# A first phase that takes the scale first and adds the shift to six of eight token tiles afterwards

## The reference, cut to what matters

```python
mod = jax.nn.silu(c) @ w_ada[l] + b_ada[l]
sh1, sc1, g1, sh2, sc2, g2 = [m[:, None, :] for m in jnp.split(mod, N_MOD, axis=-1)]
h = _rmsnorm(x, norm_g[l, 0]) * (1.0 + sc1) + sh1
z = h @ w_in
```

## Time and profile before

| | |
|---|---|
| median of 3 runs | 1763.02 us |
| lowest, highest | 1757.39, 1763.32 us |
| the profiled execution | 1760.8 us |
| its span, first to last instruction | 1759.0 us |
| PE busy | 1672.6 us, 95% |
| DVE busy | 1044.9 us, 59% |
| POOL busy | 821.6 us, 47% |
| ACT busy | 595.5 us, 34% |

### The profile page before, as it was taken

One profiled execution on the slowest core, in us unless ns is written; L12 is line 12 of the kernel. 1 busy time (PEld: TensorE's weight loads), 2 busy tenths in 40 slices (PEclk: granted clock), 3 DMA queues, 4 the chain that ended last, 5 costly groups with the idle time before them and its releaser, 6 DMA issues.

```text
span 1759.0 us, 22694 instructions
## 1 busy us (share of the span) xinstructions
PE 1672.6 (95%) x8036; PEld 1394.4 (79%) x8036; DVE 1044.9 (59%) x1746; ACT 595.5 (34%) x1054; POOL 821.6 (47%) x537
## 2 busy tenths in 40 slices
PE   2899999999999999989999999999999999999996
PEld 2787878787888888879888788888888888888884
DVE  5714835656999999947577345743453354345438
ACT  1533336264222222246323354323223222322323
POOL 0621130102446565520388423766558556755664
PEclk9999999998999999999999999999999999999998
DMA  8222141010111111240674511121112011201213
GB/s 288 86 60 60 40 110 42 31 36 32 47 58 45 45 45 51 105 102 1 221 271 160 203 61 48 37 72 48 48 48 72 25 63 55 65 30 48 72 69 158
DMA packets 37166, 138.87 MB, mean 79 GB/s; under 512 B 4592, under 2 KB 4592, under 8 KB 37104
## 3 DMA queue, kind: packets, MB, share of 16 engines
q1 hardware_dynamic: 34864, 130.70, 21.7%
q0 software_dynamic: 2240, 7.34, 1.9%
HBM read 118.10 MB, written 13.63 MB: 75 GB/s over the span
## 4 chain that ended last, share of the span: by engine, by line
PE 80%; DVE 8%; DMA 4%; issue 3%; ACT 3%; POOL 2%; SPq 0%; DVEq 0%; POOLq 0%; ACTq 0%
PE ps L612 23%; PE ps L614 23%; PE ps L613 23%; PE ps L811 4%; PE ps L790 2%; DMA region_b<-in_w_ada 2%; DVE y_f L2179 1%; PE ps L716 1%; DVE y_f L2148 1%; PE ps L717 1%; DVE region_a L2133 1%; ACT y_t L1407 1%; PE ps L642 1%; DMA raw<-in_w_ffn 1%; DVE region_a L2206 1%
## 5 line engine op out<-in xcount | busy, mean ns | idle before, releaser
L612 PE MATMUL ps<-h_t,w_t 128*128 128x512 f32 x1112 | 437.4, 393 | 0.6 <-POOL w_t L1500 0.4
L614 PE MATMUL ps<-h_t,w_t 128*128 128x512 f32 x1112 | 433.6, 390 | 0.0
L613 PE MATMUL ps<-h_t,w_t 128*128 128x512 f32 x1112 | 433.5, 390 | 0.0
L612 PEld LDWEIGHTS ps<-h_t,w_t 128*128 128x128 f32 x1112 | 209.4, 188 | 45.2 <-issue 2.4
L614 PEld LDWEIGHTS ps<-h_t,w_t 128*128 128x128 f32 x1112 | 209.2, 188 | 44.1
L613 PEld LDWEIGHTS ps<-h_t,w_t 128*128 128x128 f32 x1112 | 209.4, 188 | 42.9 <-issue 0.7
L1500 POOL TENSOR_TENSOR w_t<-raw,w_t 128x1280 fp32r<-128x1280 f32 (+1 forms) x50 | 141.6, 2832 | 196.0 <-ACT w_t L1097 195.7
L2148 DVE TENSOR_TENSOR y_f<-ps,y_f 128x512 f32<-128x512 f32 x120 | 80.7, 686 | 217.5 <-PE ps L614 217.5
L1649 POOL TENSOR_TENSOR w_t<-raw,w_t 128x512 fp32r<-128x512 f32 x80 | 110.2, 1383 | 144.5 <-ACT w_t L1388 144.4
L1833 DVE MAX8 top<-region_b 128x8 f32<-128x384 f32 (+5 forms) x192 | 157.9, 881 | 17.3 <-issue 16.7
L1836 DVE MATCH_REPLACE8 region_b<-top,region_b 128x384 f32<-128x384 f32 (+5 forms) x192 | 166.1, 876 | 0.0
(11 more groups left out here) (266 smaller groups left out, 3264.6 us busy)
## 6 DMA issues: line engine op xcount, KB each, us to landing
region_b<-in_w_ada SPq DMA_DIRECT2D x48, 512.0 KB, 4.5
raw<-in_w_ffn SPq DMA_DIRECT2D x46, 512.0 KB, 3.7
raw<-in_w_gates SPq DMA_DIRECT2D x32, 640.0 KB, 3.9
region_d<-in_w_ffn SPq DMA_DIRECT2D x20, 512.0 KB, 4.2
raw<-in_w_z SPq DMA_DIRECT2D x18, 512.0 KB, 3.6
region_a<-in_x SPq DMA_DIRECT2D x8, 512.0 KB, 11.6
raw<-in_w_o SPq DMA_DIRECT2D x8, 512.0 KB, 3.6
region_b<-in_x SPq DMA_DIRECT2D x8, 512.0 KB, 6.6
```

Of the source, the lines that this page charges most:

```text
L612: pe.matmul(o, a_hi, m_hi, start=first, stop=False, skip_group_check=more)
L613: pe.matmul(o, a_hi, m_lo, start=False, stop=False, skip_group_check=more)
L614: return pe.matmul(o, a_lo, m_hi, start=False, stop=last, skip_group_check=more)
```

## The change

- **Order of loads.** x tile 0 goes first, then the 8 blocks of the scale (into the space of h_hi, one place each), x tile 1, the value weights in four parts, x tiles 2 and 3, the 8 blocks of the shift (into w_t, raw and region_b, one place each), x tiles 4 to 7. None of them waits for a buffer. The first `w_z` load waits until the seventh shift block is used.
- **Scale first.** DVE sums only the scale before the token tiles. `mod_col[:, 0]`, the shift, starts at zero, and tiles 0 to 5 (UNSHIFTED = 6) are made without shift. Tiles 6 and 7 wait for the shift and use it.
- **Shift sums** run on DVE, two blocks after each of tiles 1 to 4.
- **Constants on PE.** `keep_busy(n)` issues n matmuls of the identity with 384 columns of constants, 7 of them while the scale comes in and 3 before the first token tile.
- **h_values** of the first phase is now shared, as it already is in the second: 4 instructions on DVE, 4 activations on ACT.
- **Value weights** in quarters: lo parts 0 and 1 on DVE ahead of `mod_col`, parts 2 and 3 on POOL after the h_lo parts of tile 0.
- **Correction afterwards.** 16 pieces of h_t (8 of 512 columns, 8 of 256) go through DVE (h_hi + shift + h_lo into `h_again`, two buffers), ACT (new h_hi) and POOL (new h_lo). z_half(0, 0) waits for the first 8, z_half(0, 1) for all 16. The values of the six tiles get the row shift·w_v: 8 plain float32 matmuls of 456 columns on PE and 6 additions on DVE, ahead of the forget logits.

```diff
+            for k in range(KT):
+                sp.dma_start(h_f[:, 0, k], w_ada[1, k]).then_inc(s_scale_in[k], 16)
...
+            for k in range(KT):
+                sp.dma_start(shift_early[k], w_ada[0, k]).then_inc(s_shift_in[k], 16)
...
+            sp.wait_ge(s_ada_used, 2 * KT - 1)
```

```diff
             def token_major(t):
-                pe.wait_ge(s_h, 2 * (t + 1))
+                pe.wait_ge(s_h, 2 * t + (1 if t == 0 else 2))
...
                     if t == 0 and k == KT // 2:
-                        pe.wait_ge(s_vw_lo[1], 1)
+                        pe.wait_ge(s_h, 2)
+                    if t == 0 and k % 2 == 0:
+                        pe.wait_ge(s_vw_lo[k // 4], k // 2 % 2 + 1)
...
+            turn_x(0)
+            for k in range(3, KT):
+                pe.wait_ge(s_scale_in[k], 16)
+                keep_busy(2 if k < 5 else 1)
+            pe.wait_ge(s_ada_used, KT)
+            modulation(1, 5)
+            turn_x(1)
             pe.wait_ge(s_mod, 2)
-            for t in range(2, TT):
-                turn_x(t)
-                token_major(t - 2)
-            token_major(TT - 2)
-            token_major(TT - 1)
+            keep_busy(3)
+            for t in range(TT):
+                token_major(t)
+                if t + 2 < TT:
+                    turn_x(t + 2)
+                if t + 3 == TT:
+                    pe.wait_ge(s_ada_used, 2 * KT)
+                    modulation(0, 6)
+            pe.wait_ge(s_shift_wide, 1)
+            for k in range(KT):
+                mm = pe.matmul(ps[:, 7, 0:VN], shift_wide[:, k], raw_v[:, k * VN:(k + 1) * VN], start=k == 0,
+                               stop=k == KT - 1)
...
+                if T == T_IDX:
+                    pe.wait_ge(s_again, KT * (half + 1))
```

ACT, in its new order:

```diff
-            for t in range(1, TT + 1):
-                h_hi_part(2 * (t - 1))
-                h_hi_part(2 * (t - 1) + 1)
-                if t + 2 < TT:
-                    x_root(t + 2)
-                if t == 3:
-                    split_hi(0)
-                if t >= 3:
-                    v_out(t - 3)
+            for t in range(TT):
+                act.wait_ge(s_mod, 4 if t >= UNSHIFTED else 2)
+                h_values(t, 2 * (t % 2) + 1, 0)
+                h_hi_part(2 * t)
+                h_hi_part(2 * t + 1)
+                if t == 0:
+                    vw_hi_part(2)
+                    vw_hi_part(3)
+                    x_root(2)
+                if t + 3 < TT:
+                    x_root(t + 3)
+                if t >= 2:
+                    v_out(t - 2)
+            split_hi(0)
+            for n in range(2 * KT):
+                k, c = again(n)
+                act.wait_ge(s_v, UNSHIFTED)
+                act.wait_ge(s_again_sum, n + 1)
+                act.activation(h_hi[:, k, c], h_again[n % 2][:, 0:c.stop - c.start], ACT.Copy).then_inc(s_again_hi, 1)
             v_out(TT - 2)
             v_out(TT - 1)
```

POOL and DVE:

```diff
             for t in range(TT):
                 h_lo_part(2 * t)
                 h_lo_part(2 * t + 1)
-                if t == 2:
-                    split_lo(0)
...
+            split_lo(0)
+            for n in range(2 * KT):
+                k, c = again(n)
+                pool.wait_ge(s_again_hi, n + 1)
+                pool.tensor_tensor(h_lo[:, k, c], h_again[n % 2][:, 0:c.stop - c.start], h_hi[:, k, c].bitcast(F32),
+                                   ALU.subtract).then_inc(s_again, 1)
```

```diff
+            for t in range(UNSHIFTED):
                 h_values(t, 0)
...
+                for k in range(shift_done, min(KT, 2 * t)):
+                    shift_sum(k)
+                shift_done = min(KT, 2 * t)
+            dve.wait_ge(s_mod, 3)
...
+            for t in range(UNSHIFTED, TT):
+                h_values(t, 0)
+            dve.tensor_copy(shift_wide, mod_col[:, 0, :].unsqueeze(2).broadcast_to((P, KT, P))).then_inc(s_shift_wide, 1)
+            dve.wait_ge(s_h, 2 * UNSHIFTED)
+            for n in range(2 * KT):
+                k, c = again(n)
+                if n >= 2:
+                    dve.wait_ge(s_again, n - 1)
+                dve.scalar_tensor_tensor(h_again[n % 2][:, 0:c.stop - c.start], h_hi[:, k, c].bitcast(F32),
+                                         mod_col[:, 0, k:k + 1], h_lo[:, k, c].bitcast(F32), ALU.add,
+                                         ALU.add).then_inc(s_again_sum, 1)
             dve.wait_ge(s_vn, TT)
+            dve.wait_ge(s_value_row, 1)
+            for t in range(UNSHIFTED):
+                dve.tensor_tensor(vn[:, t], ps[:, 7, 0:VN], vn[:, t], ALU.add).then_inc(s_values, 1)
+            dve.wait_ge(s_values, UNSHIFTED)
```

More of the change, by code:

```diff
@@ L85 @@
 MIX0 = 1
+UNSHIFTED = 6
 class Order:
@@ L195, in build @@
         raw_v = region_b[:, TT * VN:TT * VN + KT * VN]
+        shift_early = [w_f[:, k * D:(k + 1) * D] for k in range(5)] + [raw[:, 0, 0:D], raw[:, 1, 0:D],
+                                                                        region_b[:, 2 * D:3 * D]]
         ada_raw = [region_b[:, i * D:(i + 1) * D] for i in range(3)]
@@ L201, in build @@
         forget = ada_sum1
+        shift_wide = region_c[:, 0:L].rearrange("p (k n) -> p k n", k=KT)
+        h_again = [region_c[:, L + i * HALF:L + (i + 1) * HALF] for i in range(2)]
         y_s = region_c[:, :].rearrange("p (c n) -> p c n", c=BT)
@@ L218, in build @@
         vw_hi, vw_lo = (v.rearrange("p (k n) -> p k n", k=KT) for v in (vw_hi_flat, vw_lo_flat))
-        vw_half = [slice(i * KT // 2 * VN, (i + 1) * KT // 2 * VN) for i in range(2)]
+        vw_part = [slice(2 * i * VN, 2 * (i + 1) * VN) for i in range(4)]
         ys = [vw[:, i * L:(i + 1) * L] for i in range(8)]
@@ L300, in build, with again @@
         rows_of = [slice(0, HD), slice(HD, P)]
+        def again(n):
+            return n % KT, slice(0, HALF) if n < KT else slice(HALF, UNSHIFTED * P)
         def lo_halves(T):
@@ L312, in build @@
         s_raw = [sem("s_raw0"), sem("s_raw1")]
-        s_rawv = [sem("s_rawv0"), sem("s_rawv1")]
+        s_rawv = [sem(f"s_rawv{i}") for i in range(4)]
+        s_scale_in = [sem(f"s_scale_in{k}") for k in range(KT)]
+        s_shift_in = [sem(f"s_shift_in{k}") for k in range(KT)]
+        s_shift_wide = sem("s_shift_wide")
+        s_value_row = sem("s_value_row")
+        s_values = sem("s_values")
+        s_again_sum = sem("s_again_sum")
+        s_again_hi = sem("s_again_hi")
+        s_again = sem("s_again")
         s_w_hi = sem("s_w_hi")
@@ L552, in _ @@
                 for late in range(ADA_CUT[k], ADA_CUT[k + 1]):
-                    ada_load(2 * KT + late, *ADA_LATE[late])
+                    ada_load(late, *ADA_LATE[late])
                 T = T_GD + 2 + k
@@ L646, in _, with modulation @@
             pe.wait_ge(s_pack, 48)
-            for c in range(2):
-                pe.wait_ge(s_ada_used, (c + 1) * KT)
+            def modulation(c, bank):
                 for k in range(KT):
-                    mm = pe.matmul(ps[:, 5, c * KT + k:c * KT + k + 1], ada_sum1[:, c, k * P:(k + 1) * P],
-                                   ones[:, 0:1], start=True, stop=True)
-            mm.then_inc(s_mod, 1)
+                    mm = pe.matmul(ps[:, bank, k:k + 1], ada_sum1[:, c, k * P:(k + 1) * P], ones[:, 0:1],
+                                   start=True, stop=True)
+                mm.then_inc(s_mod, 1)
             def token_major(t):
-                pe.wait_ge(s_h, 2 * (t + 1))
+                pe.wait_ge(s_h, 2 * t + (1 if t == 0 else 2))
                 if t >= 2:
@@ L1133, in h_hi_part, with h_values @@
                                ACT.Copy).then_inc(s_h_hi, 1)
+            def h_values(count, bank, i):
+                act.wait_ge(s_ht, count + 1)
+                if count:
+                    act.wait_ge(s_h, 2 * count)
+                for kk in range(KT // 2, KT):
+                    ins = act.activation(h_tmp[:, kk * P:(kk + 1) * P],
+                                         ps[:, bank, (kk - KT // 2) * P:(kk - KT // 2 + 1) * P], ACT.Identity,
+                                         scale=mod_col[:, i + 1, kk:kk + 1], bias=mod_col[:, i, kk:kk + 1])
+                ins.then_inc(s_hval_act, 1)
             def square_sum(src, col, squares):
@@ L1329, in x1_root @@
                 roots(2 * TT + t, 2 * TT + t + 1, s_root)
[L1331 to L1339 removed]
             def second_h(t):
[L1342 removed]
+                h_values(TT + t, NORM_BANK[t] + 1, 2)
                 h_hi_part(2 * (TT + t))
@@ L1749, in _ @@
             dve.wait_ge(s_silu, 1)
-            for chunk in range(2):
-                for k in range(KT):
-                    ada(chunk * KT + k, k, ada_sum1[:, chunk])
-            normed_x(0)
+            order.mark(dve.memset(mod_col[:, 0, :], 0.0))
+            for k in range(KT):
+                scale_sum(k)
+                if k == 2:
+                    normed_x(0)
+            normed_x(1)
+            for i in range(2):
+                part = vw_part[i]
+                dve.wait_ge(s_vw_hi, i + 1)
```

(13 more changed lines are left out.)

125 lines of the change are left out of this document (65 added, 60 removed).

## The result

The changed kernel takes **1769.93 us** (median of 6 runs, 1767.70 to 1771.46); the kernel before, beside it, 1761.62 us (1757.39 to 1763.32). The ratio is 1.0045 with the 95% interval 1.0028 to 1.0063: slower by some 8 us. The interval excludes no change, and the size is still inside the 8.8 us that the forecast took as the band of no change. The profiled execution took 1767.7 us, its span is 1765.9 against 1759.0, so 6.9 us more. A head start of 25 us ended as a loss.

The account below looks back on a forecast made before the run. PE, working 95% of the span, was taken as the bound. z_half(1, 0) 11.5 us later plus 1.6 us of clock made 13.1 us; added to 1760.8 this gave 1773.9, predicted as 1774, range 1757 to 1786.

Parts of the forecast that it names:

- first rival: Shift sums and correction: DVE and POOL overlap after all, 1.4 us a piece, 1765 us, not slower; chance 0.25.
- Head start: At the start, the first value product begins at 27.2 instead of 52.7 us, 25.5 us early.
- The lock: DVE sums of two SBUF tensors and POOL instructions each wait for the other's whole instruction, in shift and correction sums.
- Tiles 1 to 5: From first value product to turn 7 at 70.9: 8.7 us lost, about 3.4 of it to the shift sums.
- two columns per cycle: PE's rate assumed for the constant products, at half clock; the last three end before 26 and cost nothing.
- Stop for the shift: Before tile 6, PE makes the shift columns and then idles 5.0 us; 0.9 us taken for lower clock.
- A pair of pieces: In the correction, two 512 column pieces go round DVE, ACT and POOL in 4.0 us, 256 column pairs in 2.4.
- Behind it: After the correction, v_out, six additions, logits and split_hi(1) put z_half(1, 0) at 120.0 against 108.5.
- Clock at the end: After z_half(1, 0), the lower clock costs 1.6 us more, since PE was idle almost 6 us.
- The waits it named: PE waits some 5 us before tile 6, 6 to 9, 2 to 3 and 6 before z_half(0, 0), z_half(0, 1), z_half(1, 0).
- second rival: First tiles flow at 5.83 us and the correction hides behind tiles 6, 7 and value row: 1751 us; chance 0.12.
- worse: At the start, the deep load queue delivers no faster than 300 GB/s, tiles 2 and 3 starve: 1784 us; chance 0.11.

Follow-up runs that it names:

- first experiment: The changed kernel without its 10 products of constants on PE: 1771.3 us, ratio 1.0048 to the kernel before.
- second experiment: The changed kernel with the shift's columns made on PE one turn earlier, after turn 6 instead of turn 7: 1765.28 us, ratio 1.0020 to the kernel before.
- all three repairs: The changed kernel with earlier shift columns, forget logits behind the first weight tiles and four correction buffers together: 1757.73 us, ratio 0.9975 to the kernel before.
- single repairs: The changed kernel with one edit each: shift columns a turn earlier, 1765.28 us; forget logits behind the first weight tiles, 1765.59 us; four correction buffers, 1766.34 us.

## Why the prediction was right, and where its terms were off

The change is slower, as forecast, and for the main reasons given: PE stops for the shift, then waits for a correction that goes at the pace of POOL and DVE together, then for split_hi(1) behind the logits. The size is smaller than forecast: 13.1 us became 7.6 at the score matmul and 8.3 in the medians. The measured 1769.93 is 4 us below the predicted 1774 and 5 us above the first rival's 1765, so the time by itself does not choose between them; the pieces do. And by the forecast's own limit (slower above 1771.8) the result lies in the middle band, to which it gave 0.37 and not the 0.5 of "slower". Step by step:

- **Head start, 27.2:** 27.54. Right. The constants cost nothing, right (first experiment). The last quarter was ready at 33.4 instead of 32.8.
- **The lock:** right in kind, shown by the 8-column sums and the run with the sum on ACT. The first rival, that the engines overlap, is out: it needed pieces of 1.4 us, and they took 1.94.
- **Tiles 1 to 5: this term was mis-sized.** "About 3.4 to the shift sums", turn 7 ending at 70.9; it started at 67.33, 2.7 us before the 70.0 of the forecast, and the sums cost 0.9. The forecast added one or two whole sums to a tile's chain. Of two sums only one falls between a tile's two h_lo parts and delays the pair by 1.0 us (3.5 against 2.5); the other runs while POOL is idle, or behind the pair. So the chain becomes 4.7 + 1.0 = 5.7 us, still inside PE's 5.83 a tile, and turns 4 to 7 (49.63, 55.47, 61.50, 67.33) are 5.84, 6.03 and 5.83 us apart. The forecast had named turns 5.83 us apart as a sign of being wrong; for tiles 3 to 5 it came true. The profile showed the cover, 1.1 us a tile, and the forecast did not take it off the sum.
- **Plain float32 matmuls: half their size.** The shift's columns took 1.84 us at full clock instead of 1.0, and the value row 6.28 instead of 3.1. The forecast read the 16 and the 8 records of the earlier trace rows as so many matmuls, and they are 8 and 4. Its "two columns per cycle" fails with that: 512 columns in two records of 0.43 us are four cycles a column at the higher clock. The columns cost 0.8 us at the stop. That the row cost nothing is luck: it ended at 93.88, 2.28 us before the correction let z_half(0, 0) start.
- **Stop for the shift, 5.0 us:** 4.89. **Its clock** was under-sized: 0.9 taken, but tiles 6 and 7 lasted from 74.94 to 87.60, 12.7 us instead of the forecast's 10.9. That tile 7 ends within 0.2 us of the forecast's 87.8 is this error against the earlier start. It cost nothing there, since POOL's correction set the start of z_half(0, 0), and the second experiment shows the same cover from the other side.
- **A pair of pieces, 4.0 us:** 3.88, and 2.3 instead of 2.4 for the short ones. The size was right; that 0.48 of it goes away with four buffers the forecast did not say.
- **Behind it, ACT's last copy at 107.8 to z_half(1, 0) at 120.0, 12.2 us:** 10.3 us, from 104.09 to 114.35. Six additions took 3.33 us instead of 3.9. The forecast put both tables, the exponential and the logarithm at 3.1 us behind the additions; the first load ran at 104.98, during the additions, so 1.8 us were left. That DVE's line 1914 also stands behind split_hi(1) the forecast did not see; it cost 0.3 us.
- **Clock at the end, 1.6:** 1.7.
- **The waits it named:** some 5 us before tile 6, 6 to 9 before z_half(0, 0), 2 to 3 before z_half(0, 1), 6 before z_half(1, 0). Measured: 4.89, 2.28, 3.35 and 2.06. The first is right. The second and the last are much shorter than forecast. What PE waited for came sooner, and PE came later: tiles 6 and 7 and z_half(0, 1) ran partly at the lower clock (z_half(0, 1) took 7.1 us instead of 5.5), and the value row was long.

From 120.0 to 114.35 are 5.7 us: 2.7 from the tiles, less 0.7 for the longer shift columns and their stop, 1.7 from the correction, 2.0 from the chain behind it. Most of the overestimates were lengths that had room beside them. The second rival, the head start kept, needed a correction that hides behind tiles 6 and 7; even with all three repairs PE waits 4.0 us for it. The deep queue delivered, so the case "worse" is out too.

What stays open: the size of the single repairs. The traces give 4.1, 3.9 and 5.6 us, the medians 4.7, 4.3 and 3.6, with 2.5 us of uncertainty on each and 3.1 on the changed kernel that they are compared with. Each single repair's interval overlaps that of the changed kernel (1.0028 to 1.0063); only the three together are clear of it. And what of DVE's and POOL's work overlaps in the four-buffer run was not tried apart.

## What to carry to other kernels

Take a compound change apart before timing it whole: here the loads without waits carried all the gain (9.2 us), and the part built upon them took it back twice over. Work deferred from a stage that an engine waits for has to fit into idle time of the engines that do it later, and PE must not need its result soon; ask which wait ends last after the deferral, and whether something unrelated stands behind it in program order, as split_hi(1) did behind the logits. And when a delay is added to a chain beside a bound engine, subtract the slack of that chain first.

## What the runs showed of the hardware

- A DVE sum of two tensors over 8 columns took 1.34 us beside a POOL subtraction and 0.22 alone, and a product of one tensor over 8 columns took 1.25: narrowing such an operation did not make it cheap there.
- ACT fetched its table ahead of the semaphore wait of the activation that needed it: load at 104.98, activation at 108.81, idle between.
- With four buffers a piece took 1.70 us on POOL, less than the 1.95 of the two operations alone, more than the 1.27 of one.
- After a stop of 5 us the granted clock was 0.50 and 0.53 over 71 to 81, though PE was busy all of the second half. A stop of 2.07 us before tile 2 was followed by 0.52 over 45 to 48 in one kernel's execution and by 1.00 in another's.
- The plain float32 matmuls here stand in the trace as two records each: 8 matmuls of 456 columns are 16 records and took 6.28 us, and 8 of one column took 1.84 at full clock and 3.54 at the lower one.
